# Gathered rows of the last stretch given out in 25 steps instead of 31, and a third tile finished inside the loop

## What is computed

```
q = (x @ peer_wq).reshape(T, 8, 2, 128);  s = einsum(q, peer_keys)
sv, si = top_k(s, 16)                      # in each half
top_s, pos = top_k(all sums of pairs, 16)  # 16 experts of 16384 for each of 8 heads
gate = softmax(top_s)
act  = gelu(einsum('cd,ced->ce', x, peer_u[eidx])) * gate    # 128 experts per token
out  = einsum('ce,ced->cd', act, peer_v[eidx])
y    = rmsnorm(x + gate2 * out, final_norm)
```

## Time and profile before

| | us |
|---|---|
| median of three runs | 2679.89 |
| the profiled execution, its own time | 2661.14 |
| its span, first to last instruction | 2659.3 |
| PE busy | 2362.4 (89%) |
| DVE busy | 1792.2 (67%) |
| POOL busy | 923.6 (35%) |
| ACT busy | 496.6 (19%) |

### The profile page before, as it was taken

How to read it: one execution, slowest core, us unless ns; L and a number is a source line. 1 busy time by engine, 2 the same in 40 slices (tenths; PEclk the granted TensorE clock), 3 DMA queues, 4 the chain that set the end, 5 groups by cost and what they waited for, 6 DMA issues and landing times.

```text
span 2659.3 us, 43626 instructions
## 1 busy us (share of the span) xinstructions
PE 2362.4 (89%) x18034; PEld 1651.5 (62%) x18034; DVE 1792.2 (67%) x3466; ACT 496.6 (19%) x1002; POOL 923.6 (35%) x774
## 2 busy tenths in 40 slices
PE   5989978789788888898999799998999999998997
PEld 2545536668677775333478677775776666775664
DVE  1111253345677877587699775799899898886767
ACT  2111124224444331100022210100000100000101
POOL 0000000000234442254430001667665676765653
PEclk9999988899999998999999679999999999999998
DMA  9242031120266664487894024999999999999997
GB/s 304 95 154 99 12 130 41 57 103 2 98 202 208 209 202 154 178 305 254 297 351 154 17 73 172 349 399 391 409 408 392 352 408 409 407 407 411 409 407 299
DMA packets 199455, 647.01 MB, mean 243 GB/s; under 512 B 25222, under 2 KB 27142, under 8 KB 198298
## 3 DMA queue, kind: packets, MB, share of 16 engines
q0 software_dynamic: 110592, 402.70, 40.1%
q1 hardware_dynamic: 88666, 241.52, 24.4%
HBM read 635.50 MB, written 8.65 MB: 242 GB/s over the span
## 4 chain that ended last, share of the span: by engine, by line
PE 36%; DMA 23%; DVE 22%; issue 9%; POOL 6%; ACT 4%; SPq 1%; DVEq 0%; ACTq 0%
DMA arena<-in_peer_u,arena 11%; DMA arena<-in_peer_v,arena 10%; PE ps L598 7%; POOL arena L2228 5%; PE ps L1077 3%; PE ps L1088 3%; PE ps L1099 3%; PE ps L1003 2%; DVE arena L2056 2%; PE ps L1018 2%; PE ps L600 2%; PE ps L849 2%; DVE arena L2051 1%; POOL arena L2216 1%; DVE arena L1881 1%
## 5 line engine op out<-in xcount | busy, mean ns | idle before, releaser
L1088 PE MATMUL ps<-arena 128*128 128x512 f32 x1024 | 473.6, 606 | 43.2 <-DVE arena L2095 42.9
L1077 PE MATMUL ps<-arena 128*128 128x256 f32 x2048 | 478.1, 387 | 0.0
L2228 POOL DMA_INDIRECT arena<-in_peer_u,arena x256 | 330.8, 1292 | 381.9 <-DVE arena L1848 230.8
L1077 PEld LDWEIGHTS ps<-arena 128*128 128x128 f32 x2048 | 390.8, 194 | 68.7 <-issue 19.6
L2056 DVE SCALAR_TENSOR_TENSOR arena<-arena 128x1024 f32<-128x1024 f32 x252 | 316.3, 1283 | 87.6 <-DMA arena<-in_peer_v,arena 86.7
L2228 POOL DMA_INDIRECT arena<-in_peer_v,arena x256 | 302.5, 1182 | 199.4 <-DVE arena L2056 148.5
L1088 PEld LDWEIGHTS ps<-arena 128*128 128x128 f32 x1024 | 195.8, 194 | 251.2 <-issue 245.3
L2216 POOL DMA_INDIRECT arena<-in_peer_u,arena x128 | 146.9, 1148 | 588.4 <-DVE arena L1848 320.4
L2051 DVE SCALAR_TENSOR_TENSOR arena<-arena 128x1024 bf16<-128x1024 f32 x256 | 305.4, 1222 | 47.2 <-DMA arena<-in_peer_u,arena 46.1
L1099 PEld LDWEIGHTS ps<-arena 128*128 128x128 bf16 x3072 | 206.7, 156 | 51.7 <-issue 47.7
L1099 PE MATMUL ps<-arena 128*128 128x32 bf16 x3072 | 209.6, 243 | 5.1 <-DVE arena L2088 4.0
(11 more groups left out here) (354 smaller groups left out, 3345.0 us busy)
## 6 DMA issues: line engine op xcount, KB each, us to landing
arena<-in_uT SPq DMA_DIRECT2D x128, 512.0 KB, 6.8
arena<-in_peer_v SPq DMA_DIRECT2D x128, 512.0 KB, 6.8
arena<-in_w_ada SPq DMA_DIRECT2D x12, 2048.0 KB, 14.3
arena<-in_peer_wq SPq DMA_DIRECT2D x12, 2048.0 KB, 10.3
arena<-in_w_in SPq DMA_DIRECT2D x6, 2048.0 KB, 8.0
arena<-in_w_out SPq DMA_DIRECT2D x4, 2048.0 KB, 8.8
arena<-in_peer_u,arena POOLq DMA_INDIRECT x384, 11.5
arena<-in_peer_v,arena POOLq DMA_INDIRECT x384, 11.7
```

What stands on the lines that cost most here:

```text
L1077: m = pe.matmul(ps[:, 4 + i % 2, 0:ND], us[i % UB][:, k, :], hTd[:, k, :], start=(k == 0), stop=(k == KD - 1))
L1088: m = pe.matmul(ps[:, 2 * r + c, :], sgel[:, i % SBUFS, P * r:P * r + P], vs[i % VB][:, 512 * c:512 * c + 512], start=(i == 0), stop=(i == ...
L2228: pool.indirect_dma_start(gring[:, n % RING, :], None, a[("peer_u", "peer_v")[e]][0], bass.IndirectOffsetOnAxis(ap=ids[:, t, m:m + 1], axi ...
```

## The change

The 112 rows are given to steps 96 to 120 (divisor 25). Tile 2 gets an entry in `FIN_AT` at step 122, and its parts after the loop go. Its wait for `a_ok` is for 122 instead of 128, because its buffer `yo[2]` lies over gate columns that are used up by then, and step 122 of the loop is reached before step 127.

```diff
 def rows_by(i):
-    return max(0, min(EARLY, (i - 12) * EARLY // 83)) + max(0, min(ROWS - EARLY, (i - 95) * (ROWS - EARLY) // 31))
+    return max(0, min(EARLY, (i - 12) * EARLY // 83)) + max(0, min(ROWS - EARLY, (i - 95) * (ROWS - EARLY) // 25))
-FIN_AT = {104: 0, 108: 1}
+FIN_AT = {104: 0, 108: 1, 122: 2}
@@ scalar
                 if i - 1 in FIN_AT:
                     fin_root(FIN_AT[i - 1])
-            fin_square(2)
-            fin_root(2)
             fin_square(3)
             fin_square(4)
             fin_root(3)
@@ vector, fin_sum
                 if t == 2:
-                    dve.wait_ge(S("a_ok"), ETILES)
+                    dve.wait_ge(S("a_ok"), 122)
@@ vector
                 while nr < rows_by(i):
                     gather_row(nr)
                     nr += 1
-            fin_sum(2)
-            fin_mean(2)
-            fin_norm(2)
             fin_sum(3)
```

## The result

The median of the changed kernel was 2699.39 us (six runs, 2692.87 to 2702.51) beside 2679.55 us for the kernel before; the ratio is 1.0077, with a 95% interval of 1.0064 to 1.009. A later set of runs gave 1.0095 (1.0074 to 1.0115), 2693.06 beside 2668.7 us. The profiled execution took 2692.87 us, its span is 2691.1 us. That is 31.8 us more than the span before; 4.8 us of it had passed by `weigh(96)`, where the code is still the same, and 27.0 us belong to the stretch from `weigh(96)` to the end, 272.9 us against 245.8. Lines 2056, 2060, 2095, 2108, 2110 and 2122 of the kernel before are 2054, 2058, 2093, 2106, 2108 and 2120 in this one.

A forecast was written before the change was run, and what follows sets the result against it. Full DMA engines at 409 GB/s were taken as the bound, PE close behind. Moved rows, PE's work after `weigh(121)`, the tail and a table load gave a 2682.9 us span, +23.6 on 2679.89: 2703 us, range 2692 to 2710.

The forecast's parts named there:

- The model of the stretch: `weigh(96)` to `weigh(121)` before the change: 90 rows, 50 dense loads and a 7.7 us reload at 409 GB/s take 187.2 us.
- 215.2 us to the last row, 1.26 for the addition: Steps 96 to 120: 187.0 us plus 22 moved rows at 1.282 us, then adding the accumulators ahead of `weigh(121)`.
- 38.0 us of PE's work, 0.57 to its start, 0.9 for the clock: After `weigh(121)`: delay to `back(121)`, seven backs and four hiddens without waiting, and a lower clock after PE's wait.
- Tile 2 in steps 122 to 124 costs nothing: Inside the loop, tile 2's finishing work is free because DVE has no rows left and is idle.
- the queueing: Steps 122 to 124: tile 2's root waits behind GELU(125) on ACT, delaying DVE and `weigh(125)`, with ten us of cover.
- The 1.1 us that I credited: End of the kernel: the part of tile 2's 6.6 us that was on the path, not beside `back(127)`.
- The table load in the tail, +1.4 us: Before tile 3's root: the square root's table must be loaded again, on the path; bounds 0 and 1.4 us.
- The tail: Tile 3's sum to the span's end: 12.1 us as before, plus 1.4 us for a table load.
- Rival A: Whole loop: the unchanged sum of bytes sets the end, so order does not matter; 2680 us, chance 6%.
- B: Steps 96 to 120: PE is the real bound and gathers have headroom; 5.2 us faster, 2675 us, chance 5%.
- C: Steps 96 to 120: transfers run at 431 GB/s under a denser mix of rows; +12.7 us, 2693 us, chance 6%.
- D: Steps 96 to 121: regular waits lower PE's clock, making PE the bound; +10 us more, 2713 us, chance 3%.

The follow-up runs named there:

- The control: The kernel before, run again with no edit beside itself; ratio 0.9998 (0.9986 to 1.001).

## Why the prediction was right

It forecast 2703 us, +23.6 us from the profile; measured were 2699.39 (+19.8) and +24.4 us in the second set. The mechanism was right: the moved rows lengthen the steps that receive them, and PE's 38 us of work come behind them. Step by step:

- *The model of the stretch* (rows and loads at 409 GB/s explain 187 us): right. The control repeated it, and halving the loads' bytes took 29.7 of 217.8 us away with nothing else changed.
- *215.2 us to the last row, 1.26 for the addition*: 216.5 expected, 217.8 measured, in three traces with divisor 25. In the last 10 us before `weigh(121)` the DMA engines moved only 263 GB/s, which is 3.6 us of full rate lost. The addition's 1.26 us are in it; the other 2.3 us, in which the last rows land and are used, the sum had put at nothing. About 1 us came back, since the rate up to there was 410 GB/s and 87.8 MB were moved, where the sum has 409 and 88.0.
- *38.0 us of PE's work, 0.57 to its start, 0.9 for the clock*: 39.5 expected, 41.4 measured (2636.01 to 2677.44). The `back` after the wait took 5.30 us, not 3.6, so the clock cost 1.7 us where I took the middle of 0 and 1.9; the second trace of the change has 5.2 us again, but with divisor 25 alone, behind the same wait, it cost nothing, and no run shows what decides. The other 1.1 us is a term that I had left out: the last `peer_v` load can go out only when `back(125)` is done, since there are two buffers; it took 4.2 us to land, `back(126)` takes 3.45, and `back(127)` waited 0.88 us. Before, that wait lay beneath the one for `weigh(127)`. With halved loads, where neither term occurs, the same piece took 38.7 us, and 38.0 + 0.57 is 38.6.
- *Tile 2 in steps 122 to 124 costs nothing*: right for the path. DVE waited 7.33 and 6.86 us for ACT there, as the queueing said, and PE never waited for it. What it saves at the end is also nothing: with divisor 25 alone tile 2 was done 3.9 us before tile 3 could start. The 1.1 us that I credited is the lateness of DVE in the kernel before. It goes with the rows, not with tile 2's move.
- *The table load in the tail, +1.4 us*: 1.4 us by the two traces, with and without. The root starts at 2684.85, 0.02 us after the load ends (2683.55 + 1.28), so again no further time beside the load. The Trainium skill, "ScalarE: Activation LUTs", What ACT_TABLE_LOAD costs, adds 1.38 us of drain to each switch; in these rows it does not appear.
- *The tail*, 13.5 us expected from tile 3's sum, 13.6 measured.

The sum was 3.4 us short in the stretch of the trace (27.0 against 23.6): 1.3 us of the rows, 0.8 of the clock, 1.1 of the last load. That the first median came out below the forecast, and not above it, is therefore partly luck: the medians differ by less than the stretches do, for a reason that is open. Rival A named the right resource and drew the wrong conclusion: the bytes do bound the loop, and in the divisors of 31 and over, where PE has almost no steps left behind the last row, reordering changed nothing (0.9996, 1.0004, 0.9999). It fails as soon as PE has steps left behind the last row. Rivals B and C needed rates that no full window showed. D did not come: PE waited 26 times, and the mean clock stayed at 0.98.

## What to carry to other kernels

Where two streams share full DMA engines and one of them also feeds a second engine, spread the other evenly to the very end: a transfer taken from the last steps leaves the DMA engines idle under the second engine's work, and its time is added to the steps that it is moved to. Before moving work out of a tail, look at what it lies beside; here 6.6 us of it were worth 1 us before the change and nothing after it. And when an activation function moves from behind the last use of another table to ahead of it, count a table load at the end.

## What the runs showed that I had not expected

- After a wait of PE the next `back` takes either 3.67 or 5.2 to 5.5 us, and the length of the wait does not sort them: after 1.84, 2.11 and 2.79 us it was 3.67, after 2.33, 3.10 and 8.54 us it was 5.37, 5.30 and 5.47 (all in the changed kernel). The same `back(121)` took 5.30 us after 3.10 in one kernel and 3.67 after 3.12 in another; the granted clock was 0.68 and 1.00. What decides is open.
- Kernels that are the same up to step 95 differ by up to 17 us in when they reach it (2413.5 to 2430.0 us), most of it before the loop (`weigh(0)` from 1551 to 1565 us). A stretch with a fixed mark at its start repeats to 0.5 us, while the medians of the kernel before differ by up to 12 us between sets of runs.
